# A two-block mixer kernel on one core: five of eight quads of a hidden-block pair in the seven-product form instead of four

## The reference, cut to what matters

```python
D_MODEL = 2048; SEQ = 256; D_FF = 4 * D_MODEL
...
        h2 = rmsnorm(x, norm2_g[l])
        x = x + jnp.square(jax.nn.relu(h2 @ w_mlp_in[l])) @ w_mlp_out[l]
...
        h2 = rmsnorm_2(x, g_mlp[l])
        x = x + jnp.square(jax.nn.relu(h2 @ w_up[l])) @ w_down[l]
```

## Time and profile before

| | |
|---|---|
| Median of 3 executions | 2814.95 us (2814.79 to 2814.99) |
| Profiled execution, its own time | 2815.99 us |
| Profiled execution, span from first to last instruction | 2814.3 us |
| PE busy | 2803.9 us, 13174 matmuls |
| DVE busy | 2122.4 us, 2445 instructions |
| ACT busy | 1466.5 us, 1626 instructions |
| DMA | 596.55 MB, mean 212 GB/s |

### The profile page before, as it was taken

The page is one execution under the profiler, slowest core; times in us unless marked ns, Lnnn a source line. Parts: engine busy times, 40 slices in busy tenths (PEclk is TensorE's granted clock), DMA queues, the critical chain, the costliest instruction groups (busy, mean ns, idle before and its releaser), DMA issues.

```text
span 2814.3 us, 33882 instructions
## 1 busy us (share of the span) xinstructions
PE 2803.9 (100%) x13174; PEld 2315.8 (82%) x13174; DVE 2122.4 (75%) x2445; ACT 1466.5 (52%) x1626; POOL 2.0 (0%) x7
## 2 busy tenths in 40 slices
PE   9999999999999999999999999999999999999998
PEld 7888878888888888888888888888888888888887
DVE  6697855556768787788867678877667888887786
ACT  6644446544456555555546444444455555555554
POOL 0000000000000000000000000000000000000000
PEclk9999999999999999999999999999999999999999
DMA  9576756666866666666677767667676666666674
GB/s 312 160 222 200 204 160 212 196 195 198 255 210 215 220 208 209 217 211 204 221 232 220 223 200 213 202 206 224 208 218 213 222 219 201 218 210 209 211 236 166
DMA packets 361824, 596.55 MB, mean 212 GB/s; under 512 B 22208, under 2 KB 95552, under 8 KB 361024
## 3 DMA queue, kind: packets, MB, share of 16 engines
q1 hardware_dynamic: 361232, 594.06, 67.4%
q10 hardware_dynamic: 432, 0.32, 0.0%
HBM read 556.81 MB, written 2.10 MB: 199 GB/s over the span
## 4 chain that ended last, share of the span: by engine, by line
PE 99%; DVE 0%; DMA 0%; ACT 0%; issue 0%; ACTq 0%; DVEq 0%
PE ACC L778 77%; PE TB L784 15%; PE ACC L784 6%; PE TB L898 0%; DMA SS<-in_x_t_dram 0%; PE TB L931 0%; PE TB L934 0%; PE TB L963 0%; PE TB L940 0%; PE TB L952 0%; PE TB L1003 0%; DVE WL L1518 0%; DVE SG L1877 0%; PE TB L880 0%; PE TB L976 0%; PE TB L991 0%
## 5 line engine op out<-in xcount | busy, mean ns | idle before, releaser
L1049 ACT ACTIVATE WH<-RAW 128x1024 fp32r<-128x1024 f32 (+1 forms) x1023 | 1047.7, 1032 | 1083.7 <-PE ACC L778 766.5
L1518 DVE TENSOR_TENSOR WL<-RAW,WH 128x1024 fp32r<-128x1024 f32 (+1 forms) x1023 | 1197.5, 1187 | 411.3 <-ACT WH L1049 408.7
L778 PE MATMUL ACC<-WH,XTH 128*128 128x512 f32 (+1 forms) x1692 | 658.2, 389 | 0.0
L778 PE MATMUL ACC<-WL,XTH 128*128 128x512 f32 (+1 forms) x1692 | 655.2, 387 | 0.0
L778 PE MATMUL ACC<-WH,XTL 128*128 128x512 f32 (+1 forms) x1692 | 655.2, 387 | 0.0
L778 PEld LDWEIGHTS ACC<-WH,XTH 128*128 128x128 f32 x1692 | 317.7, 188 | 66.0 <-DVE WL L1518 0.4
L778 PEld LDWEIGHTS ACC<-WH,XTL 128*128 128x128 f32 x1692 | 317.7, 188 | 65.1
L778 PEld LDWEIGHTS ACC<-WL,XTH 128*128 128x128 f32 x1692 | 317.8, 188 | 63.9
L778 PE MATMUL ACC<-WH,YAH 128*128 128x512 f32 x864 | 336.2, 389 | 0.0
L778 PE MATMUL ACC<-WL,YAH 128*128 128x512 f32 x864 | 336.2, 389 | 0.0
L778 PE MATMUL ACC<-WH,YAL 128*128 128x512 f32 x864 | 336.1, 389 | 0.0
(11 more groups left out here) (335 smaller groups left out, 2786.5 us busy)
## 6 DMA issues: line engine op xcount, KB each, us to landing
RAW<-in_w_in_dram SPq DMA_DIRECT2D x255, 512.0 KB, 4.4
RAW<-in_w_mlp_in_dram SPq DMA_DIRECT2D x128, 512.0 KB, 4.6
RAW<-in_w_mlp_out_dram SPq DMA_DIRECT2D x128, 512.0 KB, 4.8
RAW<-in_w_up_dram SPq DMA_DIRECT2D x128, 512.0 KB, 4.5
RAW<-in_w_down_dram SPq DMA_DIRECT2D x128, 512.0 KB, 4.7
RAW<-in_w_gate_dram SPq DMA_DIRECT2D x96, 512.0 KB, 4.5
YT<-HT SPq DMA_DIRECT2D x208, 128.0 KB, 3.3
RAW<-in_w_branch_dram SPq DMA_DIRECT2D x48, 512.0 KB, 4.2
```

What stands on the lines that cost most here:

```text
L778: ins = e.matmul(ACC[:, 2 * (b % 2) + half, 0:n], p[:, k, xs], q[:, t, 0:n], start=(k == 0 and m == 0), stop=(k == nk - 1 and m == 2))
L1049: e.activation(WH[u % NSPL][:, ts, 0:n], RAW[u % NRAW][:, ts, 0:n], ACT.Copy).then_inc(hi, 1)
L1518: e.tensor_tensor(l, r, h, ALU.subtract).then_inc(lo, 1)
```

## The change

`SEVEN_I` becomes (0, 2, 3, 5, 6) in the later pairs, and the first pair of each MLP has three such quads (`FIRST_I`, at i = 0, 2, 5). A list `QUADS` holds each quad's pair and the index of its x forms. Quads 2, 3 and 5, 6 are now neighbours. The parts of the weight sums take three places in turn instead of two (`t_pair`; the third, TX, is new memory), so that the first part of a quad waits for the quad two before and only the second for the quad just before; in the second quad of two neighbours (`CLOSE`) the second part comes one unit later, behind the next unit's cut. The sums of x have five columns of tiles instead of four, the form S_3 in a buffer of its own (G3), and the buffers YT of the turned tiles now share the memory of HB. The splits of a pair's turned tiles come nine and ten units behind the pair's last unit; before it was 12 and 14 (3 + 9 and 5 + 9). Some waits ask for the split (`turn_lo`) where they asked for the turning.

```diff
-    SEVEN_I = (0, 2, 4, 6)
+    SEVEN_I = (0, 2, 3, 5, 6)
+    FIRST_I = (0, 2, 5)
     units, U0, UE = [], [0] * len(plan), [0] * len(plan)
-    PAIR, SEVEN = {}, {}
+    PAIR, SEVEN, QUADS = {}, {}, []
...
-                    if i in SEVEN_I:
-                        SEVEN[u] = (4 * PAIR[u][0] + SEVEN_I.index(i), m)
+                    if i in (SEVEN_I if name[1] > 1 else FIRST_I):
+                        if m == 0:
+                            QUADS.append((PAIR[u][0], SEVEN_I.index(i)))
+                        SEVEN[u] = (len(QUADS) - 1, m)
                 units.append((b + m, i))
     NU = len(units)
     SEVEN_END = [u for u, (q, m) in SEVEN.items() if m == 1]
+    PAIR_END = [max(u for u in SEVEN_END if PAIR[u][0] == n) for n in range(14)]
+    QUADS1 = sum(n < 7 for n, _ in QUADS)
+
+    CLOSE = [u for u in SEVEN_END if u - 2 in SEVEN_END]
...
+    G3 = [sb(f"G3{n}", [P, 4, P], F32R, forms) for n in "HL"]
...
+    TX["1"] = sb("TX1", [P, 4, 512], F32R, m1)
...
+    YT["1"] = [h[:, :, :].rearrange("p a (t n) -> p (a t) n", t=4) for h in HB["1"]]
...
+    def t_pair(tag, q, k, part):
+
+        r = (2 * q + k) % 3
+        return TX[tag][:, 2 * part:2 * part + 2, :] if r == 2 else TS[part][:, 2 * r:2 * r + 2, :]
+
+    def x_form(tag, f, s, part):
+        if f == S_4:
+            return S4R[tag][part][:, s, :]
+        if f == S_3:
+            return G3[part][:, s, :] if s < 4 else SXR[part][:, 15, :]
+        return SXR[part][:, 5 * f + s, :]
...
-                turn_at(("h" + tag, j, b), end + 3 + 2 * b, 9)
+                turn_at(("h" + tag, j, b), end + 3 + 2 * b, 6 - b)
...
-                e.wait_ge(xs_lo, 2 * (n // 7) + 2)
+                e.wait_ge(xs_lo, 3 * (n // 7) + 3)
...
-            new, end = q % 4 == 0, q % 4 == 3
+            new, end = QUADS[q][1] == 0, u - m == PAIR_END[n] - 1
 
             def sums(f):
-                return [y[:, f, q % 4, :] for y in SXR] if f != S_4 else [y[:, q % 4, :] for y in S4R[tag]]
+                return [x_form(tag, f, QUADS[q][1], part) for part in range(2)]
 
             def weight_sums(f):
-                return [y[:, f, :] for y in TS]
+                return [t_pair(tag, q, f // 2, part)[:, f % 2, :] for part in range(2)]
...
-        def sums_high(u):
-            q = SEVEN[u][0]
-            tr = TR[NAMES[units[u][0]][0][1]]
-            if q:
-                e.wait_ge(mm, SEVEN_END[q - 1] + 1)
-            for k in range(2):
-                e.wait_ge(t_sum, 4 * q + 2 * k + 2)
-                e.activation(TS[0][:, 2 * k:2 * k + 2, :], tr[:, 2 * k:2 * k + 2, :], ACT.Copy).then_inc(t_hi, 1)
+        def sums_high(u, k):
+            q, tag = SEVEN[u][0], NAMES[units[u][0]][0][1]
+            if q >= 2 - k:
+                e.wait_ge(mm, SEVEN_END[q - 2 + k] + 1)
+            e.wait_ge(t_sum, 4 * q + 2 * k + 2)
+            e.activation(t_pair(tag, q, k, 0), TR[tag][:, 2 * k:2 * k + 2, :], ACT.Copy).then_inc(t_hi, 1)
...
-                if SEVEN.get(u + AHEAD, (0, 0))[1]:
-                    sums_high(u + AHEAD)
+                if u + AHEAD - 1 in CLOSE:
+                    sums_high(u + AHEAD - 1, 1)
+                if u + AHEAD in SEVEN_END:
+                    sums_high(u + AHEAD, 0)
+                    if u + AHEAD not in CLOSE:
+                        sums_high(u + AHEAD, 1)
...
+                e.wait_ge(turn_lo, 2 * TN[{"1": "x1", "2": "x3"}[tag], 2 + b] + 2)
...
-                e.wait_ge(turned, TN["h" + tag, j - 1, 0] + 1)
-                e.wait_ge(mm, SEVEN_END[4 * n + 3] + 1)
+                e.wait_ge(turn_lo, 2 * TN["h" + tag, j - 1, 0] + 2)
+                e.wait_ge(mm, PAIR_END[n] + 1)
...
-        def weight_sums_low(u):
-            q, tr = SEVEN[u][0], TR[NAMES[units[u][0]][0][1]]
-            if q:
-                e.wait_ge(mm, SEVEN_END[q - 1] + 1)
-            for k in range(2):
-                f = slice(2 * k, 2 * k + 2)
-                e.wait_ge(t_hi, 2 * q + k + 1)
-                e.tensor_tensor(TS[1][:, f, :], tr[:, f, :], TS[0][:, f, :], ALU.subtract).then_inc(t_lo, 1)
+        def weight_sums_low(u, k):
+            q, tag = SEVEN[u][0], NAMES[units[u][0]][0][1]
+            if q >= 2 - k:
+                e.wait_ge(mm, SEVEN_END[q - 2 + k] + 1)
+            e.wait_ge(t_hi, 2 * q + k + 1)
+            e.tensor_tensor(t_pair(tag, q, k, 1), TR[tag][:, 2 * k:2 * k + 2, :], t_pair(tag, q, k, 0), ALU.subtract).then_inc(t_lo, 1)
...
-                if SEVEN.get(u + AHEAD, (0, 0))[1]:
-                    weight_sums_low(u + AHEAD)
+                if u + AHEAD - 1 in CLOSE:
+                    weight_sums_low(u + AHEAD - 1, 1)
+                if u + AHEAD in SEVEN_END:
+                    weight_sums_low(u + AHEAD, 0)
+                    if u + AHEAD not in CLOSE:
+                        weight_sums_low(u + AHEAD, 1)
...
+            e.tensor_tensor(sx[S_1], AX[:, :, 0, 1, :], AX[:, :, 1, 1, :], ALU.add).then_inc(xs, 1)
+            e.tensor_tensor(sx[S_3], sx[S_A][:, 0:4, :], AX[:, 0:4, 0, 1, :], ALU.subtract).then_inc(xs, 1)
+            e.tensor_tensor(FGB[tag][:, 15, :], sx[S_A][:, 4, :], AX[:, 4, 0, 1, :], ALU.subtract).then_inc(xs, 1)
...
+            e.tensor_tensor(S4R[tag][1], sx[S_4], S4R[tag][0], ALU.subtract).then_inc(xs_lo, 1)
+            e.tensor_tensor(G3[1][:, :, :], sx[S_3], G3[0][:, :, :], ALU.subtract).then_inc(xs_lo, 1)
```

More of the change, by code:

```diff
@@ L221, in build @@
     ST = sb("ST", [P, 160])
+    forms = ExitStack()
+    G3 = [sb(f"G3{n}", [P, 4, P], F32R, forms) for n in "HL"]
+    forms.close()
     GBP = sb("GBP", [P, 2, 512])
@@ L303, in build @@
     m1 = ExitStack()
-    YB, HB, XB, HT, YT, S4R = {}, {}, {}, {}, {}, {}
+    YB, HB, XB, HT, YT, S4R, TX, TXF = {}, {}, {}, {}, {}, {}, {}, {}
     YB["1"] = sb("YBH1", [P, 8, L], F32R, m1), sb("YBL1", [P, 8, L], F32R, m1)
+    sums1 = ExitStack()
+    TXF["1"] = sb("TXF1", [P, 16, P], F32, sums1)
+    sums1.close()
+    TX["1"] = sb("TX1", [P, 4, 512], F32R, m1)
+    HT["1"] = [sb(f"HT{i}1", [P, 4, 2, P], F32, m1) for i in range(2)]
     HB["1"] = [sb(f"HB{i}1", [P, 2, 512], F32, m1) for i in range(2)]
-    HT["1"] = [sb(f"HT{i}1", [P, 4, 2, P], F32, m1) for i in range(2)]
-    YT["1"] = [sb(f"YT{i}1", [P, 8, P], F32, m1) for i in range(2)]
+    YT["1"] = [h[:, :, :].rearrange("p a (t n) -> p (a t) n", t=4) for h in HB["1"]]
     XB["1"] = sb("XBH1", [P, 16, L], F32R, m1), sb("XBL1", [P, 16, L], F32R, m1)
     FG = sb("FG", [P, D], F32, m1)
-    S4R["1"] = sb("S4H1", [P, 4, P], F32R, m1), sb("S4L1", [P, 4, P], F32R, m1)
+    S4R["1"] = sb("S4H1", [P, 5, P], F32R, m1), sb("S4L1", [P, 5, P], F32R, m1)
     m1.close()
@@ L347, in build @@
     YB["2"] = sb("YBH2", [P, 8, L], F32R, m2), sb("YBL2", [P, 8, L], F32R, m2)
+    sums2 = ExitStack()
+    TXF["2"] = sb("TXF2", [P, 16, P], F32, sums2)
+    sums2.close()
+    TX["2"] = sb("TX2", [P, 4, 512], F32R, m2)
+    HT["2"] = [sb(f"HT{i}2", [P, 4, 2, P], F32, m2) for i in range(2)]
     HB["2"] = [sb(f"HB{i}2", [P, 2, 512], F32, m2) for i in range(2)]
-    HT["2"] = [sb(f"HT{i}2", [P, 4, 2, P], F32, m2) for i in range(2)]
-    YT["2"] = [sb(f"YT{i}2", [P, 8, P], F32, m2) for i in range(2)]
+    YT["2"] = [h[:, :, :].rearrange("p a (t n) -> p (a t) n", t=4) for h in HB["2"]]
     XB["2"] = sb("XBH2", [P, 16, L], F32R, m2), sb("XBL2", [P, 16, L], F32R, m2)
-    S4R["2"] = sb("S4H2", [P, 4, P], F32R, m2), sb("S4L2", [P, 4, P], F32R, m2)
+    S4R["2"] = sb("S4H2", [P, 5, P], F32R, m2), sb("S4L2", [P, 5, P], F32R, m2)
     m2.close()
-    AX = XTF[:, 2048:4096].rearrange("p (s k r t) -> p s k r t", s=4, k=2, r=2)
+    AX = XTF[:, 1536:4096].rearrange("p (s k r t) -> p s k r t", s=5, k=2, r=2)
     FGS = {"1": FG, "2": FG2}
-    SX = {tag: f[:, :].rearrange("p (f s t) -> p f s t", f=4, s=4) for tag, f in FGS.items()}
-    SX4 = JK[:, :].rearrange("p (s t) -> p s t", s=4)
+    FGB = {tag: f[:, :].rearrange("p (b t) -> p b t", t=P) for tag, f in FGS.items()}
+    SX = {tag: [f[:, 5 * i:5 * i + 5, :] for i in range(3)] + [TXF[tag][:, 0:4, :], TXF[tag][:, 4:9, :]] for tag, f in FGB.items()}
     TR = {tag: f[:, :].rearrange("p (f n) -> p f n", f=4) for tag, f in FGS.items()}
     XTHF, XTLF = (x[:, :, :].rearrange("p k t -> p (k t)") for x in (XTH, XTL))
-    SXR = [x[:, 0:2048].rearrange("p (f s t) -> p f s t", f=4, s=4) for x in (XTHF, XTLF)]
+    SXR = [x[:, 0:2048].rearrange("p (b t) -> p b t", t=P) for x in (XTHF, XTLF)]
     TS = [x[:, 2048:4096].rearrange("p (f n) -> p f n", f=4) for x in (XTHF, XTLF)]
+    def t_pair(tag, q, k, part):
[7 more added lines that the diff above has]
+        return SXR[part][:, 5 * f + s, :]
     T1, T2, T3, T4 = range(4)
@@ L624, in _ @@
                         e.wait_ge(c_done, 6)
+                    if g == "g2b":
+                        multiplied(e, "h1", 7, 1)
                     e.dma_start(GB[n % 2], row(GBIAS[g][512 * c:512 * c + 512], 512)).then_inc(ld_gb[n % 2], 16)
@@ L1361, in sums_split @@
             multiplied(e, "wo" + tag, 3)
-            e.wait_ge(xs, 11 * int(tag))
```

(27 more changed lines are left out.)

17 lines of the change are left out of this document (7 added, 10 removed).

## The result

The changed kernel takes **2820.44 us** (median of 22 executions, 2818.66 to 2823.09); the kernel before took 2815.32 us in as many (2814.54 to 2816.22). The ratio is 1.0018, 95% interval 1.0012 to 1.0024: slower by 0.18%, just inside the 0.2% that the forecast called no change. Thirty matmuls fewer bought nothing.

What follows compares the result with a forecast made beforehand. PE, busy 2803.9 of 2814.3 us, was taken as the bound, with DVE's queue deciding its stall in later pairs. 12 x (0.88 - 0.90) + 0.84 = +0.6 us on the 2814.95 us median gave 2815.5 us, range 2805 to 2824.

Steps and rivals of the forecast that it cites:

- Part 1: PE's matmuls: 30 fewer, 6.8 us less; a later period becomes 83.64 us plus its stall, against 84.54.
- Part 2: PE's wait for the residual add at a0 and a1: earlier splits remove this stall, 0.22 us a pair.
- Part 3: DVE's queue through a0 to a13 in later pairs: ends at 34.03 us, where PE wants its result at 33.32.
- S: PE's stall per later pair at T3, T4 of quad 6, from DVE's late end: 0.71 + 0.17 = 0.88 us.
- The own waits: In DVE's queue, sums of quads 3 and 6 wait for the low part directly before: 0.115 us each, 0.23.
- The gap: DVE's wait for tile a11 before the sums of quad 5: 0.51 us, bounds 0 and 1.81.
- Part 4: Work behind DVE's queue: ACT's high parts, a15's cut, SP's queue and the new waits for splits cost nothing.
- Part 5: The two first pairs: three more matmuls each and a stall of 0.25 us, so +0.42 us each, +0.84.
- Part 6: Five columns of x forms: about 2.4 us more on DVE per MLP, hidden in its idle time, so nothing.
- A: Rival: PE's count alone decides, with no stall if DVE's queue ends by 33.15; 2805.0 us, chance 0.22.
- B: Rival: DVE's wait for its own low part just before is free; 2812.8 us, chance 0.12.
- C: Rival: tile a11 lands later, slowing PE at quad 6 from a gap of 0.93 us on; 2821.2 us, chance 0.25.

Runs made afterwards that it cites:

- cut_first_add: Changed kernel with each quad's first-tile cut before its sums (except i=0) and an o-block's last residual add one unit later on DVE; 2805.03 us.
- four_quads: Changed kernel with four seven-product quads (0, 2, 4, 6) in every pair, keeping the other parts of the change; 2812.45 us.
- old_splits: Changed kernel with the splits of the turned tiles back at their old units, 12 and 14 behind the pair; 2837.79 us.
- no_a11_load: Changed kernel without the load of tile a11 (second block, i=5) in the twelve later pairs, so some weights are left out; 2812.24 us.
- two_places: Changed kernel with two places for the parts of the weight sums, as before the change, instead of three; 2846.71 us.
- cut_first_a11: Changed kernel with DVE's cut of a10 in front of the weight sums of the quad at i=5, all work kept; 2812.62 us.
- own_wait: Changed kernel with DVE's wait before a quad's sums split, so the first sum waits for a low part one instruction further back; 2815.81 us.
- cut_first_all: Changed kernel with the cut of a quad's first tile in front of its sums, for every quad but that at i=0; 2808.27 us.

## Why the prediction was right, and where it was off

The time was forecast as 2815.5 (range 2805 to 2824), no change; it is 2820.44, no change by the bound given, and 4.9 us above the point. That it still counts as no change is in part luck: 5.1 us of the 5.6 allowed are used up, and the interval, 1.0012 to 1.0024, reaches over the bound.

- **Part 1, the matmuls.** Right: 30 fewer, and cut_first_add shows them worth their pitch where nothing else stalls.
- **Part 2, the old stall.** Right, and shown: it is 0 in four_quads and comes back as the same row in old_splits. The add starts at +0.20.
- **Part 3, DVE's queue.** Right in mechanism and place; S was mis-sized, 0.88 against 1.13. The missing 0.25 is made up as follows. The own waits cost 0.17 each, not 0.115, which gives 0.11: I took the price from a wait behind a sum of 512 columns, and this one stands behind a part of 1024. The gap of 0.52 idle, forecast as 0.51, moves the queue by some 0.07 more than its idle time: the starts at 1306.69 and 1308.30 are 1.61 apart, 0.47 above the pitch, for 0.39 idle. PE's restart costs 0.20, not 0.17. The remaining 0.04 is not traced. My sum without the gap, 33.29 + 0.23, was 33.52; with 0.17 a wait it is 33.63, and no_a11_load measured 33.62. "The same time, not more" for the stop at a12 holds: PE loses 0.11 on the matmul behind that stop too, but the wait for T3 takes it back, since DVE's end sets when that wait is over (see no_a11_load).
- **Part 4, behind it.** Right: no waits for the new places. two_places shows what the third one saves, 3.3 - 1.1 = 2.2 us a pair.
- **Part 5, the first pairs.** +0.65 and +0.56 against +0.42: the same direction, and inside its bounds. Of the 0.46 us of stall in the first one, 0.23 lies at a2, the third unit, in every kernel with these first pairs, and 0.19 at a10, whose cut stands behind the wait for a11; I had allowed 0.25 in all. In cut_first_a11 the second part is gone (41.76 and 41.74 us).
- **Part 6, the forms of x.** Right as far as seen: the MLP starts no later than before.

Twelve times 0.25 us and twice 0.18 make 3.4 of the 4.9 us; the rest is in the scatter of this kernel, which spreads over 4.4 us.

**The rivals.** A, PE's count alone, was worked out at 2805.0 for a queue that ends by 33.15. The changed kernel's ends at 34.24; put in another order it ends at 32.90, and the time is 2805.03. B fell with own_wait. The rule it came from (the Trainium skill, VectorE: DVE Perf Modes, The DRAIN you can't avoid, that a semaphore on chained operations "costs nothing extra here", measured there on eight tensor_copy) does not hold for the tensor_tensor of this kernel: a wait on the instruction just before costs 0.17 us behind 1024 columns, which own_wait shows, and the pitch behind 512 is longer by 0.11 where there is such a wait. C, a11 landing later: the wait for it stood in every later pair, but the gap reached C's bound of 0.93 us in two of the twelve only, and its mean was as forecast. The measured time is close to C's 2821.2, but it did not come about in C's way.

What the prediction did not see is an order, not a price. It found the wait for a11 and costed it rightly, but did not ask what ready work was queued behind that wait. The cut of a10 was. Exchanging the two at quad 5 takes the mean stall from 1.13 to 0.66 us. In quads 3 and 6 the same exchange also parts the sums from the low part that they wait for, which saves the two own waits, and the stall is 0.24, with all of the work kept.

## What to carry to other kernels

When an edit cuts the bound engine's work and the time stays, lay out the helper engine's queue through the stretch by starts, and find its end against the moment the bound engine asks; here that sum was right to 0.2 us in 34. Then look at each wait in that queue for ready work behind it: an instruction that needs nothing of the awaited tile goes in front, where it hides the landing and parts an instruction from the one that it must wait for. Only after that is a further shift of work onto the helper (the fifth quad) worth its saved matmuls: 2805.03 us here, against 2812.45 with four quads and no stall in the later pairs.

## What the runs showed of the hardware that was not expected

- A DVE instruction that waits for the one just before it starts 0.17 us later (1024 columns: pitch 1.31 against 1.135), and at no cost if one other instruction stands between (own_wait: 1.135 again).
- A stop of PE costs more than its wait: the matmul behind the first one is 0.11 us late as well, at each stop. But of two stops on the way to the same late part the first costs nothing more: the stall was DVE's end - 33.32 + 0.17 to 0.23 with a stop at a12 and without.
- A DMA landing on the path seems to show in the scatter as well as in the mean. With it the executions spread over 4.4 us (22 of them); without it over 0.8 us (four_quads, 10; cut_first_add, 5) and 1.5 us (no_a11_load, 10). That this is the cause is not shown: cut_first_all, with at most 0.2 us of that gap left, still spreads over 3.0 us (10). Within one execution DVE's idle time for the landing of a11 went from 0.27 to 0.99 us from pair to pair.
